# Four resident experts in 24 pieces of 8 KB, and a closing norm shared by two engines, in a streaming encoder step with a mixture of experts

## What is computed

```python
proj = rms_norm(x) @ w_in                      # 1024 x 7168
... two gated convolution mixers, merged, @ w_o, added to x
xn = rms_norm(x, norm2_g)                      # 384 x 1024
grp = top-1 of 4 groups ; top_i = top-2 of the 8 experts of that group ; combine = their weights
for e in range(32):
    hdn = silu(xn @ w_gate[e]) * (xn @ w_up[e])        # 1024 x 512 each
    out = out + combine[:, e:e + 1] * (hdn @ w_down[e])    # 512 x 1024
y = rms_norm(x + out, final_norm_g)
```

## Time and profile before

| | us |
|---|---|
| median of 3 runs | 863.28 (861.98 to 864.88) |
| the profiled execution | 860.66 |
| its span, first to last instruction | 858.9 |

### The profile page before, as it was taken

One profiled execution on the slowest core, in us unless ns is written; L12 is line 12 of the kernel. 1 busy time (PEld: TensorE's weight loads), 2 busy tenths in 40 slices (PEclk: granted clock), 3 DMA queues, 4 the chain that ended last, 5 costly groups with the idle time before them and its releaser, 6 DMA issues.

```text
span 858.9 us, 21583 instructions
## 1 busy us (share of the span) xinstructions
PE 777.0 (90%) x8655; PEld 592.4 (69%) x8656; DVE 426.4 (50%) x1142; ACT 321.3 (37%) x556; POOL 258.4 (30%) x129
## 2 busy tenths in 40 slices
PE   3999999999999999989999688999989879989963
PEld 3999999999999998865555344555545545555532
DVE  4046977999994034253444323544434425434524
ACT  5333767464336923332322212233222312322213
POOL 3846699978486878100000000000000000000000
PEclk9999999999999999988999989999999999999997
DMA  7734343435445548824899999999999999999992
GB/s 250 222 101 146 99 148 98 148 98 168 142 138 189 205 147 290 295 85 187 364 424 422 421 422 423 422 422 422 422 422 422 422 422 421 422 422 422 422 421 107
DMA packets 53173, 250.01 MB, mean 291 GB/s; under 512 B 6599, under 2 KB 6599, under 8 KB 28561
## 3 DMA queue, kind: packets, MB, share of 16 engines
q1 hardware_dynamic: 49184, 244.86, 72.1%
q10 hardware_dynamic: 3953, 4.67, 1.9%
HBM read 246.76 MB, written 2.75 MB: 290 GB/s over the span
## 4 chain that ended last, share of the span: by engine, by line
PE 61%; DMA 21%; DVE 11%; ACT 3%; issue 2%; SPq 2%; POOL 1%; DVEq 0%
PE bank L1323 24%; DMA ring<-in_exp_w_up 20%; PE bank L1492 12%; DVE bank L1001 7%; PE bank L1521 7%; PE bank L1480 5%; PE bank L1443 5%; PE bank L1321 4%; SPq L523 2%; PE bank L1508 1%; PE bank L1450 1%; DMA raw<-in_w_in 1%; DVE sq L1063 1%; ACT w_hi L692 1%; PE bank L1384 1%
## 5 line engine op out<-in xcount | busy, mean ns | idle before, releaser
L1492 PE MATMUL bank<-ring,xe 128*32 128x256 f32 x2816 | 170.0, 392 | 43.5 <-DMA ring<-in_exp_w_up 35.0
L571 POOL TENSOR_TENSOR w_lo<-raw,w_hi 128x2048 fp32r<-128x2048 f32 x40 | 184.9, 4625 | 75.3 <-ACT w_hi L692 75.2
L1492 PEld LDWEIGHTS bank<-ring,xe 128*32 128x32 f32 x2816 | 97.7, 113 | 109.9 <-issue 60.7
L1323 PE MATMUL bank<-x_hi,w_hi 128*128 128x384 f32 x448 | 150.9, 337 | 1.5 <-POOL w_lo L571 1.3
L1323 PE MATMUL bank<-x_hi,w_lo 128*128 128x384 f32 x448 | 149.7, 334 | 0.0
L1323 PE MATMUL bank<-x_lo,w_hi 128*128 128x384 f32 x448 | 149.7, 334 | 0.0
L1001 DVE SCALAR_TENSOR_TENSOR bank<-ub,vec,bank 128x256 f32<-128x256 f32 (+1 forms) x416 | 137.1, 414 | 0.0
L1232 DVE SCALAR_TENSOR_TENSOR hid<-bank,slot_coef,sig 64x256 f32<-64x256 f32 x44 | 21.5, 489 | 182.9 <-ACT sig L874 182.9
L692 ACT ACTIVATE w_hi<-raw 128x2048 fp32r<-128x2048 f32 x40 | 76.6, 1918 | 83.1 <-PE bank L1323 71.4
L1521 PE MATMUL bank<-ring,hidT 128*32 128x256 f32 x1408 | 94.2, 384 | 5.6
L1323 PEld LDWEIGHTS bank<-x_hi,w_hi 128*128 128x128 f32 x448 | 84.1, 188 | 2.9 <-POOL w_lo L571 1.5
(11 more groups left out here) (228 smaller groups left out, 980.2 us busy)
## 6 DMA issues: line engine op xcount, KB each, us to landing
ring<-in_exp_w_gate SPq DMA_DIRECT2D x64, 1024.0 KB, 24.6
ring<-in_exp_w_up SPq DMA_DIRECT2D x64, 1024.0 KB, 26.3
ring<-in_exp_w_down SPq DMA_DIRECT2D x64, 1024.0 KB, 26.3
raw<-in_w_in SPq DMA_DIRECT2D x28, 1024.0 KB, 5.1
raw<-in_w_out_a SPq DMA_DIRECT2D x4, 1024.0 KB, 5.0
raw<-in_w_out_b SPq DMA_DIRECT2D x4, 1024.0 KB, 5.1
raw<-in_w_o SPq DMA_DIRECT2D x4, 1024.0 KB, 5.2
out<-n_tok ACTq DMA_DIRECT2D x3, 512.0 KB, 2.7
```

Source lines behind the costliest of these rows:

```text
L571: pool.tensor_tensor(w_lo[u % NW][:, :, :], raw[u % NW][:, :, :], w_hi[u % NW][:, :, :].bitcast(F32), ALU.subtract).then_inc(lo_ready, 1)
L1323: ins = pe.matmul(b, wp[:, k % UK, cols], xp[:, k, :], start=start, stop=stop)
L1492: last = pe.matmul(GU[q * T:(q + 1) * T, :], xe[:, k, :], wide(slots[q // 2])[:, k, q % 2 * QE:(q % 2 + 1) * QE], start=(k == 0), stop=(k ...
```

## The change

- `ring` becomes 24 pieces of 8 KB per partition (`piece`), each with its own semaphore; `SETS` names two pieces for each of three matrices of four sets. Memory for the fourth set comes from laying things over each other: the convolution buffer, `merged`, `ua`, `ub`, `x_tok`, `stage` and the constants of the router lie under pieces, the item loop's buffers (`pick`, `xe`, `hidT`, `y_lo`, `table`) in the lower half of `x2T`, `at_slot`, `back_to` and `y_hi` over `tmp`, the router's scratch. The reserved area at address 0 shrinks from 16384 to 1024 bytes per partition. The pieces begin at byte 32736 of a partition; the ring began at 16512.
- `first_weights` now loads 24 pieces, for places 0 to 3. One is issued before unit 30 of the first stage, four after units 32 to 35 as before, three where there were two after `CHUNK_END[NCH - 3]`; 20 are issued when the last `Wo` group is done (before: 16), one more after the last logits, and the last three after `combined` is 1 and the tables are ready (before: two).
- The loops of SyncE and TensorE go round 8 times with four experts (before: 10 times with three, and two experts behind). SyncE loads the expert four places ahead. Experts 0 to 3 keep the first four places.
- GpSimd clears `y_hi`, `y_lo` and `back_to` only after the last router table has been read.
- End: rows are taken in the order 1, 2, 0 (`LAST_ORDER`), the first after two of three turns of `combine`. ScalarE squares one half (with the scale 1/32, so that the sum is a mean) while VectorE multiplies the other by `gf`; then VectorE takes mean and inverse, and both engines scale one half each. SyncE issues the stores. `gf` is loaded by SyncE after the last expert's weights, once TensorE has done the gate and up part of place 28.

```diff
-    SETS = ((6, 7, 5), (4, 0, 2), (1, 3, 8))
-    RING = 9
+    SETS = (((15, 16), (17, 18), (20, 9)), ((10, 11), (12, 1), (2, 0)),
+            ((4, 7), (5, 8), (3, 6)), ((13, 14), (19, 21), (22, 23)))
+    NSETS = len(SETS)
+    LAST_ORDER = (1, 2, 0)
...
+        piece = [at(f"piece{i}", [P, 2048], F32, halves_at + UNIT * i) for i in range(HALVES)]
+        n_out = at("n_out", [P, NT, D], F32, halves_at + UNIT * SETS[0][0][0])
+        gf = at("gf", [P, D], F32, halves_at + UNIT * SETS[0][1][0])
...
             for u in range(UNITS):
+                if u == 30:
+                    first_weights(0, 2, 0)
...
             sp.wait_ge(grp_done, CHUNK_END[X_LO_USED])
+            first_weights(0, 2, 1)
+            sp.wait_ge(grp_done, CHUNK_END[NCH - 3])
+            first_weights(1, 0, 0)
             first_weights(1, 0, 1)
-            sp.wait_ge(grp_done, CHUNK_END[NCH - 3])
-            first_weights(0, 2, 0)
-            first_weights(0, 2, 1)
+            first_weights(1, 1, 0)
...
             sp.wait_ge(grp_done, len(GROUPS))
-            first_weights(2, 0, 1)
-            first_weights(2, 1, 0)
+            first_weights(2, 2, 0)
+            first_weights(2, 2, 1)
+            first_weights(3, 0, 0)
+            first_weights(3, 0, 1)
+            sp.wait_ge(aux_done, aux("logit", NT - 1) + 1)
+            first_weights(3, 1, 0)
             sp.wait_ge(stage_out[0], 80)
+            sp.wait_ge(stage_out[1], 16)
             sp.wait_ge(x_rows_ready, NT)
             sp.wait_ge(ssq_ready, 2 * NT)
+            sp.wait_ge(tables_ready, 1)
             sp.wait_ge(combined, 1)
-            first_weights(2, 2, 0)
-            first_weights(2, 2, 1)
+            first_weights(3, 1, 1)
+            first_weights(3, 2, 0)
+            first_weights(3, 2, 1)
...
+            with sp.Fori(1, NE // NSETS) as rnd:
+                for side in range(NSETS):
+                    last_item = sp.value_load(table[0:1, bass.ds(rnd * NSETS + (side + 1 - NSETS), 1)],
+                                              min_val=1, max_val=MAX_ITEMS)
...
+            last_item = sp.value_load(table[0:1, NE - NSETS + 1:NE - NSETS + 2], min_val=1, max_val=MAX_ITEMS)
+            sp.wait_ge(gate_up_done, last_item)
+            sp.dma_start(gf[:, :], final_g.rearrange("(a d) -> a d", a=1).to_broadcast([P, D])).then_inc(g_in, 16)
...
+            act.wait_ge(combined, items * NT + NT)
+            last_square(0, 0)
+            last_square(0, 1)
             act.wait_ge(combined, items * NT + (NT + 1))
...
+            last_square(1, 0)
+            last_square(1, 1)
+            root(0)
+            last_square(2, 0)
+            root(1)
+            last_square(2, 1)
+            scale(0)
+            root(2)
+            scale(1)
+            scale(2)
...
+            dve.wait_ge(combined, items * NT + NT)
+            weight(0, 1)
+            weight(0, 0)
+            dve.wait_ge(combined, items * NT + (NT + 1))
+            weight(1, 1)
+            weight(1, 0)
+            mean_square(0)
+            mean_square(1)
+            inverse_root(0)
+            weight(2, 1)
+            scale(0)
+            inverse_root(1)
+            weight(2, 0)
+            mean_square(2)
+            scale(1)
+            inverse_root(2)
+            scale(2)
```

More of the change, by code:

```diff
@@ L304, in trunk_program @@
         merged_lo_ready = sem("merged_lo_ready")
-        weights_in = [[sem(f"weights_in{i}_{h}") for h in range(2)] for i in range(RING)]
+        weights_in = [sem(f"weights_in{i}") for i in range(HALVES)]
         consts = sem("consts")
@@ L431, in trunk_program @@
         turned = [scratch(P, 3 * NT), scratch(P, 2 * NT)]
-        slot_rem = scratch(2 * NT).rearrange("p (c i) -> p c i", c=2)
         cnt = scratch(1, NE)
@@ L522, in expert_weights @@
                     src = w_dn if c == 2 else w_gu[c]
-                    sp.dma_start(ring[slot][:, h * 2048:(h + 1) * 2048],
-                                 src[bass.ds(e, 1), h, :, :].rearrange("e p x -> p (e x)"))\
-                      .then_inc(weights_in[slot][h], 16)
-            sp.wait_ge(tables_ready, 1)
-            with sp.Fori(1, NE // 3) as rnd:
-                for side in range(3):
-                    last_item = sp.value_load(table[0:1, bass.ds(rnd * 3 + (side - 2), 1)], min_val=1, max_val=MAX_ITEMS)
-                    e = sp.value_load(table[0:1, bass.ds(rnd * 3 + (side + NE + 1), 1)], min_val=0, max_val=NE - 1)
-                    expert_weights(e, side, last_item)
@@ L898, in _, with last_square @@
-            for i in range(NT):
-                act.wait_ge(normed, NT + i + 1)
-                dst = y_prompt[0, i * P:(i + 1) * P, :] if i < NP // P else y_sample.rearrange("s t d -> (s t) d")
-                act.dma_start(dst, n_tok[:, i, :]).then_inc(y_out, 16)
-            act.wait_ge(y_out, 16 * NT)
+            def last_square(n, h):
+                i = LAST_ORDER[n]
+                if n or h:
+                    act.wait_ge(ssq_ready, 2 * NT + 2 * n + h)
+                if h:
+                    act.wait_ge(weighted, 2 * n + 1)
+                at_col = (16, 42)[h] + i
+                act.activation(squares[:, :], total(i, h)[:, :], ACT.Square, scale=1.0 / ROOT_D,
+                               accum_out=small[:, at_col:at_col + 1]).then_inc(ssq_ready, 1)
@@ new lines, in root, with scale @@
+            def root(n):
+                i = LAST_ORDER[n]
+                act.wait_ge(root_in, 4 + n)
+                act.activation(small[:, 24 + i:25 + i], small[:, 20 + i:21 + i], ACT.Sqrt).then_inc(root_out, 1)
+            def scale(n):
+                i = LAST_ORDER[n]
+                act.wait_ge(scale_ready, n + 1)
+                act.wait_ge(weighted, 2 * n + 2)
+                act.activation(n_out[:, i, 0:HALF], n_out[:, i, 0:HALF], ACT.Copy, scale=small[:, 28 + i:29 + i])\
+                   .then_inc(normed_by_act, 1)
@@ L1266, in _, with weight @@
[L1266 to L1275 removed]
+            def weight(n, h):
+                i, cols = LAST_ORDER[n], slice(h * HALF, (h + 1) * HALF)
+                if h == 0:
+                    dve.wait_ge(ssq_ready, 2 * NT + 2 * n + 1)
+                dve.tensor_tensor(n_out[:, i, cols], total(i, h)[:, :], gf[:, cols], ALU.mult).then_inc(weighted, 1)
@@ L1530, in _, with experts @@
             seed(0, 0).then_inc(combined, 1)
-            bounds = [pe.alloc_register(f"bound{c}") for c in range(4)]
-            def experts(e, n, filled):
-                pe.reg_load(bounds[0:n + 1], table[0:1, bass.ds(e, n + 1)])
-                at_item = [pe.snap(x, min_val=0 if c == 0 else 1, max_val=MAX_ITEMS) for c, x in enumerate(bounds[0:n + 1])]
-                for side in range(n):
+            bounds = [pe.alloc_register(f"bound{c}") for c in range(NSETS + 1)]
+            def experts(e, filled):
+                pe.reg_load(bounds, table[0:1, bass.ds(e, NSETS + 1)])
+                at_item = [pe.snap(x, min_val=0 if c == 0 else 1, max_val=MAX_ITEMS) for c, x in enumerate(bounds)]
+                for side in range(NSETS):
                     with pe.Fori(at_item[side], at_item[side + 1]) as i:
                         item(i, SETS[side], filled)
-            with pe.Fori(0, NE // 3) as rnd:
-                experts(rnd * 3, 3, rnd * 16 + 16)
-            experts(NE // 3 * 3, NE % 3, NE // 3 * 16 + 16)
+            with pe.Fori(0, NE // NSETS) as rnd:
+                experts(rnd * NSETS, rnd * 16 + 16)
             items = pe.value_load(table[0:1, NE:NE + 1], min_val=NE, max_val=MAX_ITEMS)
```

237 lines of the change are left out of this document (121 added, 116 removed).

## The result

The changed kernel takes **850.24 us** (median of 4 runs, 847.72 to 850.97) where the kernel before took 862.63 us beside it (4 runs, 860.87 to 864.88). The ratio is 0.986, 95% interval [0.984, 0.988]: 12.4 us faster. Forecast were 847.4 us and 15.9 us off; the time lies inside the range of 844.5 to 852.5, and 3.5 us of the gain are missing. The profiled execution of after took 847.72 us with a span of 845.2 us, against 860.66 and 858.9 before, so the two traces differ by 13.7 us of span. They agree with the medians (12.4 us) closely enough to be compared term by term; the execution traced is the quickest of the four of after.

A forecast was written before the change was run, and what follows sets the result against it. The item loop was taken to be bound by the stream of expert weights. Gains of 14.9 us (stream) and 1.0 us (end) made 15.9 us off 863.28, so 847.4 us, range 844.5 to 852.5.

The forecast's parts named there:

- Bound and mechanism: Item loop: bound by the stream of expert weights at 14.92 us an expert, against 12.4 us on TensorE.
- Six pieces fewer, 14.9 us: Stream after the second hole: 162 pieces left instead of 168, at 2.487 us each, 14.9 us less.
- Rival A: Weight stream: 1% slower at the new addresses, costing 4.0 us, 851.4 us in all; chance 0.11.
- If the first stage ends at another time than 363 us, the new layout or the early piece reaches it, which I cost at nothing: First stage: layout and the piece before unit 30 were taken to cost 0; another end time would show otherwise.
- rival B: Start of the item loop slips, so the hole before 402 us moves; 7.5 us lost, 854.9 us; chance 0.07.
- a first loop load after 403 us: SyncE's first load in the item loop: forecast at about 402 us; later than 403 meant the loop's start slipped.
- Pieces into idle time: Before the loop: six extra pieces fit idle DMA time at no cost, the last three ending near 399.2 us.
- Loops of four: Item loop's rounds and exit: fewer round ends gain nothing, the exit costs 0 to 0.5 us, taken as 0.
- The end: After the last expert: rows reordered, work shared, stores queueing; gain 1.0 us, bounds 0 and 2.1.
- TensorE's waits for weights: Item loop: of 35.0 us waiting for expert weights, about 15 go and 20 stay.
- The range: Whole kernel: 844.5 to 852.5 us, meant to hold 8 in 10.
- the forecast's own 845 to 849.5: Whole kernel: range without the rivals, from the end's -2.1 to +1 us and 1.5 us of median noise.

The follow-up runs named there:

- e6_hold: Against e5_ctrl: the six pieces of place 3 requested only once TensorE has used the first halves of place 0; 862.6 us, ratio to before 1.001.
- e4: Kernel before with ring, weights and `x_hi` 96 B further up, all at 224, and e1_ctrl's loads of the bounds; 865.9 us, ratio 1.0045.
- e8: Against e5_ctrl: pieces and `x_hi` both moved to a multiple of 256 B; 843.4 us, ratio to before 0.978.
- e9: Kernel before with `x_hi` and pieces moved to a multiple of 256 B, and e5_ctrl's load of the bounds; 856.8 us, ratio 0.996.
- e10: Against e5_ctrl: `x_hi` and tiles around it moved to 224 past a multiple of 256 B, pieces staying at 224; 850.6 us, ratio to before 0.987.
- e11: Against e5_ctrl: the piece issued ahead of unit 30's load is issued late in the first stage instead; 852.4 us, ratio to before 0.990.
- e7_old_end: Against e5_ctrl: the old end, ScalarE squares all halves and its queue stores, VectorE weights and scales; 853.6 us, ratio to before 0.991.
- e2_align256: Against e1_ctrl: a pad moves the pieces to a multiple of 256 B, `x_hi` stays at 128; 852.7 us, ratio to before 0.990.
- e5_ctrl: Control: changed kernel with TensorE's five bounds of a round loaded at once by a helper that checks their range; 852.1 us, ratio to before 0.989.
- e1_ctrl: Control: changed kernel with TensorE's five bounds of a round loaded one by one, each with limits; 852.3 us, ratio to before 0.989.
- e3_align128: Against e1_ctrl: a pad moves the pieces to 128 past a multiple of 256 B, where `x_hi` stands; 849.4 us, ratio to before 0.985.

## Why the prediction was right or wrong

**Bound and mechanism: right.** The item loop is bound by the stream, and what counts is how many pieces are left after the second hole. e6_hold shows it: keep everything of the change but the early start of six pieces, and the time is that of before.

**Six pieces fewer, 14.9 us: the count right, the rate off by 0.3%.** "Rival A" came true in small. The pieces' rows start 224 B past a multiple of 256 instead of 128, and a piece takes 2.487 us instead of 2.479: over 162 pieces 1.2 us. A rate off by 0.3% is 8% of the gain, since the gain is 6 pieces and the rate works on 162. I had noted that every load of before went to one layout and still took the rate unchanged, because it was flat whatever piece was written. That flatness said nothing: all places of the ring stood a multiple of 256 B apart and shared one remainder. e4, e8, e9 and e10 show that the remainder alone sets the rate, in either kernel: 2.447, 2.479, 2.487 at 0, 128, 224.

The page "DMA: Bandwidth & Descriptors" of the Trainium skill, section "How a descriptor splits into AXI transactions", makes a start past a multiple of 256 B cost the beats in front of it. The direction agrees with the runs, the sizes only in part. An estimate by that page: from 0 to 128 four beats on some 260, 1.5%, measured 1.3%; from 128 to 224 three more, 1.2%, measured 0.3%. The page says it of what a transfer reads; here the source stays and the place that is written moves.

**"If the first stage ends at another time than 363 us, the new layout or the early piece reaches it, which I cost at nothing": this is the term that failed, put at nothing**. The stage is 2.05 us longer; it started 0.26 us earlier in after, so it ends 1.8 us later, and 1.5 are left at item 0 and 1.13 at the second hole's load. The sign given for rival B, a first loop load after 403 us, came up with it (403.06). It was the layout, not the early piece (e11). With `x_hi` and the weights' tiles at another distance within 256 B than 0, a matmul of the first stage takes on average 336 to 341 ns instead of 334 to 337. Matmuls overlap about twofold (192 in 33.5 us are 175 ns each), so 4 + 3 + 2 ns on 448 each, 4.0 us of busy time, are some 2 us of the stage. The delay grows over the stage, which a late load wouldn't give. First of before, then of after, the stage's first block in the chain and the matmuls of the low parts of the two mixers' outputs with their weights (x count, busy us, mean ns of one):
```profile
19.11 33.56 PE bank L1323 x192
```
```profile
L1323 PE MATMUL bank<-cva_lo,w_hi 128*128 128x384 f32 x64 | 21.4, 334 | 0.0
```
```profile
18.85 33.84 PE bank L1402 x192
```
```profile
L1402 PE MATMUL bank<-cva_lo,w_hi 128*128 128x384 f32 x64 | 21.7, 339 | 0.0
L1402 PE MATMUL bank<-cvb_lo,w_hi 128*128 128x384 f32 x64 | 21.4, 334 | 0.0
```
In after `cva_lo` stands beside `x_hi`, 96 B off the weights, and takes 339 ns; `cvb_lo` stands under the pieces like the weights, at a distance of 0, and takes 334. The blocks say the same: the first, with `x_hi`, is 0.28 us longer, and that of `Wo` (330.04 before, 331.23 after) 0.61, while the 192 matmuls at 296.49 and 297.71, whose operands all stand under the pieces in after, take 33.55 and 33.52 us: there the delay stands still. e10, which moves `x_hi` and the tiles beside it and leaves the pieces, takes it away. The trace of before had one distance and couldn't show it. Why the distance costs time stays open. The means of single kinds don't tell it either: `x_lo` stands among the weights in every kernel, and yet `x_lo,w_hi` goes from 334 to 336 ns at 96 and down to 332 at 128, so overlapping matmuls pass time to one another, and only their sum is sure. Of the rivals, B named a slip of the loop's start but for other reasons; its conditions (`tables_ready`, `stage_out`, clears) weren't late, since TensorE doesn't wait in front of item 0 in the chain of after. The part of the start that the clock has: item 0's first 64 matmuls take 4.12 us where before has 4.46.

**Pieces into idle time: right.** 20 pieces were issued by 366.6 us, the 21st about 373.5, the last three from 391.5 on. They ended at about 401.6 us, not 399.2, so the cover was 1.5 us where I had 2.7; it was TensorE, not they, that set 403.06.

**Loops of four: right at 0.** TensorE waits 5.9 us in 7 gaps for a round's start, against 8.6 in 8. From the last second half to VectorE's last `y_lo` it is 8.34 us, before 8.33: leaving the loop costs nothing.

**The end: right, 1.16 against 1.0 us.** Timeline of the kernel after:
```profile
832.27 0.42 DVE L1303 TENSOR_TENSOR y_lo<-bank,y_hi 128x256 fp32r<-128x256 f32 x1
...
838.03 0.48 DVE L1334 TENSOR_SCALAR n_out<-n_out,small 128x512 f32<-128x512 f32 x1
...
838.80 0.71 ACT L938 ACTIVATE n_out<-n_out,small 128x512 f32<-128x512 f32 x1
...
839.53 1.65 SPq L566 DMA_DIRECT2D out<-n_out  x3
```
The first store is issued 15.60 us after the last second half started, before 16.55: 0.95 earlier where I said 0.7. The scales took 0.48 and 0.71, not 0.4 and 0.6. All three stores go out within 1.65 us instead of 3.16, and their bytes queue, as worked out: the page has 3.3 us to landing, before 2.7. e7_old_end gives 1.4 us for this edit. `gf` was never what an engine waited for: issued at 805.91 us, it landed 24.1 us later, about 830, 4 us before its first use.

**TensorE's waits for weights: wrong, 26.4 us where I said near 20.** I took the whole gain out of that one wait. The loop got 14.0 us shorter (446.5 to 432.5 us from item 0 to the last half), and of that 8.6 came out of this wait, 2.7 out of the gaps between rounds, and the rest from the pace of TensorE. The end isn't touched by how a slack is divided.

**The range held the time**, since it reached to A for 0.11 of the chance; 850.24 us lies above the forecast's own 845 to 849.5. That it came so near to A's 851.4 is luck: of A's 4.0 us the stream lost 1.2, while 1.1 came from the first stage, which A doesn't name, and 0.7 from time outside the span. The range's lower half was out of reach once both addresses moved.

## What to carry to other kernels

Where a stream of loads is the bound, move loads into idle time and count what is left after the last hole; that count times the measured rate gave the length of the stretch to within 0.3%, and the gain to 8% (13.7 us for 14.9). When a change moves buffers, work out each address modulo 256, of the rows that DMA writes, and the distance of the two operands of the hot matmuls to each other: here a pad of 160 B and a smaller scratch area are worth 8.7 us, where the six pieces of the fourth set were worth 10.5 (e6_hold). A rate that is the same in all rows of one trace says nothing of a layout that the trace doesn't have.

## What the runs showed of the hardware

- **The start of a row in SBUF sets the rate of a load.** With rows of 8 KB: 427 GB/s at a multiple of 256 B, 422 at 128 past it, 420 at 224 past it.
- **The distance of the first stage's operands modulo 256 B sets its pace.** With `x_hi` at a distance of 0 from the weights the stage takes 343.5 to 343.7 us, whether both stand at 0, 128 or 224; at 96 it takes 345.7, at 128 (e2_align256) 346.6. The three kinds of matmuls take 337, 334 and 334 ns at 0 (335 for the last two in e8_all_256), 341, 337 and 336 at 96, 344, 338 and 332 at 128.
- **A short stop of TensorE can cost more than itself.** The clock stood at 0.50 (1.2 of 2.4 GHz) ahead of item 0 with and without a stop. With 1.09 us of waiting it came back later, and place 0 came free 13.7 us after the start of item 0 instead of 11.6: the stop cost 1.1 us and the clock 2.1 more. At the end, 32 matmuls took 1.93 us at 1.00 in the execution of after, and 3.06 us in that of e5_ctrl (3.56 in e8_all_256), where the clock had fallen to 0.50. The longer stops right ahead don't explain it, since e8_all_256 had the shorter ones.
- **TensorE's slack is thin.** Seen as a mean it is 12.4 of 14.9 us an expert; but 3.8 us of loads at a round's start left 0.5 us of waits for pieces (e1_ctrl), and with them TensorE was the bound in e2_align256 and e3_align128.
